# Shifting kinds of items against each other in one program order: a hybrid GLA / DeltaNet / MLA block on one core

## What is computed

```python
for l in range(DEPTH):                                  # DEPTH = 2
    h  = rmsnorm(x, norm_w) * (1 + scale) + shift       # scale, shift, gate from silu(c) @ ada_w
    p  = h @ w_in                                       # all branches' columns at once
    ya = gated_head_norm(bidirectional(gla_chunk_scan, ...), gla_norm_w, p['gla_z'])
    # GDN: 5-tap conv over tokens, silu, l2norm of q and k, then per chunk of 64 tokens
    #   t_inv = inverse(eye + strict_lower((k*beta) @ k.T * decay)); u = t_inv @ v_beta; w = t_inv @ ...
    #   v_new = u - w @ s;  o = q @ s + att @ v_new;  s = s * d + k.T @ v_new
    yb = gated_head_norm(bidirectional(gdn_chunk_scan, ...), gdn_norm_w, p['gdn_z'])
    yc = softmax(qn @ kn.T + qr @ kr.T) @ v * silu(p['mla_z'])        # low-rank q and kv
    x  = x + gate * (sum_i sigmoid(p['merge_gate'][i]) * (y_i @ w_branch[i])) @ w_out
```

## Time and profile before

| | us |
|---|---|
| median of 3 executions | 2361.31 (2359.95 to 2364.90) |
| the profiled execution's own time | 2353.64 |
| its span, first to last instruction | 2351.6 |
| TensorE busy | 2167.6 (92% of the span) |
| VectorE, ScalarE, GpSimd busy | 931.7, 846.4, 358.0 |
| mean granted TensorE clock | 0.969 |
| HBM traffic over the span | 80 GB/s |

### The profile page before, as it was taken

How to read it: one execution, slowest core, us unless ns; L and a number is a source line. 1 busy time by engine, 2 the same in 40 slices (tenths; PEclk the granted TensorE clock), 3 DMA queues, 4 the chain that set the end, 5 groups by cost and what they waited for, 6 DMA issues and landing times. The chain is left out here.

```text
span 2351.6 us, 31435 instructions
## 1 busy us (share of the span) xinstructions
PE 2167.6 (92%) x10970; PEld 1468.8 (62%) x10970; DVE 931.7 (40%) x2271; ACT 846.4 (36%) x2205; POOL 358.0 (15%) x591
## 2 busy tenths in 40 slices
PE   6999899899979989999999999988988968899998
PEld 3676576555545776555674437766575657766787
DVE  2023364656563325333331120246667653243321
ACT  2223253535443224444231112245346443244421
POOL 1000007071542000000000010000742760000000
PEclk8999899999989999999999999999999989999999
DMA  8215312211212022111222342122321312223243
GB/s 290 68 58 171 101 39 66 80 51 47 81 28 64 28 63 82 55 46 37 73 73 89 107 149 77 34 73 67 95 64 55 89 38 73 63 92 110 90 143 126
DMA packets 191419, 190.14 MB, mean 81 GB/s; under 512 B 28559, under 2 KB 185955, under 8 KB 190755
## 3 DMA queue, kind: packets, MB, share of 16 engines
q1 hardware_dynamic: 186048, 171.08, 23.5%
q0 software_dynamic: 3648, 16.72, 2.2%
q10 hardware_dynamic: 1571, 0.34, 0.1%
HBM read 178.62 MB, written 9.50 MB: 80 GB/s over the span
## 5 line engine op out<-in xcount | busy, mean ns | idle before, releaser
L1042 PE MATMUL bank<-hT,ring 128*128 128x512 f32 (+2 forms) x1856 | 727.1, 542 | 5.5 <-DMA ring<-in_w_in_dram 3.5
L1042 PEld LDWEIGHTS bank<-hT,ring 128*128 128x128 f32 (+1 forms) x1856 | 335.4, 192 | 256.1 <-issue 237.7
L1042 PE MATMUL bank<-ring,hT 128*128 128x256 f32 (+2 forms) x2112 | 458.5, 373 | 25.0 <-DMA ring<-in_w_in_dram 25.0
L1042 PE MATMUL bank<-WORK 128*128 128x128 f32 (+4 forms) x3056 | 403.7, 289 | 73.8 <-ACT WORK L1672 21.0
L1042 PEld LDWEIGHTS bank<-WORK 128*128 128x128 f32 (+3 forms) x3056 | 324.9, 172 | 188.9 <-issue 139.4
L1042 PEld LDWEIGHTS bank<-ring,hT 128*128 128x128 f32 x2112 | 385.8, 193 | 88.1 <-issue 35.6
L1042 PE MATMUL bank<-yT,ring 128*128 128x512 f32 (+1 forms) x768 | 273.4, 490 | 0.0
L1042 PEld LDWEIGHTS bank<-yT,ring 128*128 128x128 f32 x768 | 139.5, 193 | 80.2 <-issue 71.1
L1007 POOL TENSOR_TENSOR WORK<-WORK 64x31 f32<-64x31 f32 (+15 forms) x248 | 149.5, 603 | 19.4
L1977 DVE SCALAR_TENSOR_TENSOR WORK<-WORK,CW 128x512 f32<-128x512 f32 (+1 forms) x192 | 146.7, 764 | 3.0
L1005 POOL TENSOR_TENSOR WORK<-WORK 64x31 f32<-64x31 f32 (+15 forms) x248 | 139.5, 562 | 19.5
(11 more groups left out here) (202 smaller groups left out, 2071.0 us busy)
## 6 DMA issues: line engine op xcount, KB each, us to landing
ring<-in_w_in_dram SPq DMA_DIRECT2D x92, 1024.0 KB, 5.4
ring<-in_ada_w_dram SPq DMA_DIRECT2D x24, 1024.0 KB, 6.4
ring<-in_w_branch_dram SPq DMA_DIRECT2D x24, 1024.0 KB, 5.2
ring<-in_w_out_dram SPq DMA_DIRECT2D x8, 1024.0 KB, 5.0
ring<-in_mla_q_up_dram SPq DMA_DIRECT2D x8, 576.0 KB, 4.0
xs<-yT POOLq DMA_DIRECT2D x2, 2048.0 KB, 10.6
ring<-in_mla_kv_up_dram SPq DMA_DIRECT2D x8, 512.0 KB, 4.7
yT<-xs POOLq DMA_DIRECT2D x2, 2048.0 KB, 10.0
```

The source lines that it names most:

```text
L1042: return nc.tensor.matmul(o, a, b, start=start, stop=stop, skip_group_check=True)
```

## The change

A table gives some kinds of items a number, and the finished plan is sorted by position minus that number: a kind with 5 stands five positions ahead of its even place, one with -3 three behind. Items without an entry keep theirs, and equal keys stay in the old order. Keys that begin with v are for the VectorE part of a split kind. The banks, the ring and SyncE's issues are worked out from the new plan by the same rules. Besides, the first `gqk` product of a layer, which is woven with `lr`, now waits for its own block of shifted input by itself, as `lr` did; before, it relied on standing behind `lr`. The items are the same 2422, with the same instructions.

```diff
--- before.py
+++ after.py
@@ -149,6 +149,20 @@
 def pieces(it):
 
     return [("pc",) + it + (i,) for i in range(NPIECE[it[0]] - 1)] + [it]
+
+
+AHEAD = {'gw': 4, 'ga': 2, 'dnq': 3, 'yT': -2, 'cv': 4, 'ms': 2, 'mkv': 3, 'muk': -6, 'dx6': 3, 'dqkv': 5, 'd1': 1, 'muq': 2, 'dya': 3, 'vdn': -2, 'gv': 4, 'ab': 4, 'go': -3, 'dn': -1, 'mo': -8, 'vdsil2': 1, 'abT': -7, 'sq': -3, 'nx': 3, 'dy6': 3, 'dv': 1, 'dyb': 2, 'mod': -1}
+
+
+def settle(s):
+
+    def at(n):
+        it = s[n]
+        mark, it = (it[0], it[1:]) if it[0] == "v" else ("", it[1:-1] if it[0] == "pc" else it)
+        g = it[2] if it[0] in PHASE and PHASE[it[0]] < 2 and len(it) > 2 else 0
+        return n - AHEAD.get((mark + it[0], it[1], g), AHEAD.get(mark + it[0], 0))
+
+    return [s[n] for n in sorted(range(len(s)), key=lambda n: (at(n), n))]
 
 
 def schedule():
@@ -346,7 +360,7 @@
         if sums:
             s += sums[6:7] + [("mod", l + 1, 4)] + sums[7:] + [("modT", l + 1, 4), ("mod", l + 1, 5), ("modT", l + 1, 5)]
     s += [("xout", tt, h) for tt in tiles(DEPTH - 1) for h in range(2)]
-    return s
+    return settle(s)
 
 
 PHASE = {"lr": 0, "gqk": 0, "gv": 0, "ga": 0, "ge": 0, "gb": 0, "gatt": 0, "gw": 0, "go": 0,
@@ -760,6 +774,13 @@
                 else:
                     for who in READERS[b[0]]:
                         pe.wait_ge(*done(b, who))
+
+        def input_here(pe, l, kk):
+
+            if kk in SHIFTED_BY_DVE[l]:
+                pe.wait_ge(s_hd, shifted(l, kk, True))
+            else:
+                pe.wait_ge(s_ha, shifted(l, kk, False))
 
         def rows_of(u):
             return {"kup": KVL // P, "qup": QL // P}.get(u[0], KT)
@@ -1101,10 +1122,7 @@
                     w = weights(it)
                     n = KT // (last_piece + 1)
                     for kk in range(piece * n, piece * n + n):
-                        if kk in SHIFTED_BY_DVE[l]:
-                            pe.wait_ge(s_hd, shifted(l, kk, True))
-                        else:
-                            pe.wait_ge(s_ha, shifted(l, kk, False))
+                        input_here(pe, l, kk)
                         grp = kk % NGRP_LR
                         ins = mm(ps[grp * 32:(grp + 1) * 32, :], w[:, kk, :], hT[:, kk, :],
                                  kk < NGRP_LR, kk >= KT - NGRP_LR)
@@ -1123,6 +1141,8 @@
                     w = weights(it)[:, :, (j % 2) * P:(j % 2 + 1) * P]
                     n = KT // (last_piece + 1)
                     for kk in range(piece * n, piece * n + n):
+                        if k == "gqk" and it[2] == 0:
+                            input_here(pe, l, kk)
                         ins = mm(ps[:, a0:T], w[:, kk, :], src[:, kk, a0:T], kk == 0, kk == KT - 1)
                 elif k in ("gv", "z", "mkv", "mq"):
```

## The result

The changed kernel takes 2287.86 us (median of 4, 2285.61 to 2291.36) against 2360.63 for the kernel before (median of 4), 72.8 us less by the two medians. The prediction had 32 and a range that ended at 2300. The direction was right and the size wrong by a factor of two. In a later comparison on another chip the same kernel stood at 0.9728 (0.9713 to 0.9742), 64 us. One execution of the kernel with `mkv` alone, the one that was traced, took 2407 us at a mean clock of 0.922; it is left out of that kernel's ratio, and its trace is not read.

A forecast was written before the change was run, and what follows sets the result against it. TensorE was taken as the bound, its idle and low-clock time the only gain. Terms of 41 us gained less 9 lost made 32: 2321.6 us for a profiled execution, 2329 for the median, range 2300 to 2354.

The forecast's parts named there:

- Bound: Whole kernel: TensorE is the bound; only its idle and lower-clock time can be won, nothing between 1000 and 1390 us.
- Norm products: Conv products: waits before `dn` shrink 15.9, restarts 3.6; 4 lost before `d2`, 5 beside the solve; net 10.5 us gained.
- Loads: `w_in` loads: moving `mkv` ahead frees ring slots sooner for `mq` and `z`; 8 of 28.5 us gained.
- Tail before the scan: Head pair 2: the last silu and ScalarE's copy for the scan come sooner; 4.5 us gained.
- Inversion: Head pairs' inversion: `dy6` one filler further from `dx6` gains 3.6, `dya` behind `dx` loses 2; 1.5 us gained.
- MLA and yT: MLA: `mo` later gains 7.4, `mkT` loses 2.5, so 5 us gained; `yT` two places later gains 2.5.
- What gets later: New waits: `sq` behind `st` 2, `abT` near `dg` 1, `ab` at layer 1's GDN entry 3, unseen 3; 9 us lost.
- Clock: TensorE: four spells at lower clock follow waits that shrink, so they shrink too; 7 us gained.
- More goes than I count: Rival, chance 0.09: all norm waits, half the loads and more elsewhere vanish; 55 us gained, 2306 us.
- The waits only move: Rival, chance 0.23: TensorE, once earlier, meets the same head, solve or scan landings; 10 us gained, 2351 us.
- The slower one: Rival, chance 0.09: beside GpSimd's solve, VectorE's taps make the conv chain the bound, period above 8.60; 15 us slower, 2376.

The follow-up runs named there:

- the conv group: Only the six entries dqkv, cv, dnq, dn, v.dn, v.dsil2 in the table, against the kernel before: ratio 0.9882, 28 us gained.
- the inversion's entries: Only dx6 3, dy6 3, dyb 2, dya 3, dv 1, d1 1 in the table, against the kernel before: ratio 0.9956, 10 us gained.
- the last versions: Changed kernel with head pair 2's first `st` 12 ahead (both layers; layer 0 only; both, last silu chain 12 later): 0.9726, 0.9731, 0.9714 of before.
- `mo` and its neighbours: Only mo -8, muk -6, muq 2, ms 2 in the table, against the kernel before: ratio 0.9939, 14 us gained.
- the entry's four: Only ab 4, abT -7, nx 3, mod -1 in the table, against the kernel before: ratio 0.999 (0.9977 to 1.0002).

## Why the prediction was wrong in size

The mechanism held: TensorE's waits went where the plan moved them. The step that failed is the pricing of the terms. The idle time that the trace lists was taken for the whole price of a wait outside the norm products, loads were followed behind `mkv` alone, the inversion was priced for one of its steps, and 9 us of losses were put in that hardly came.

**Bound.** Right. TensorE's work did not change, the full stretch around 1000 to 1390 stayed full, and the gain came out of TensorE's waits but for a few us of clock.

**Norm products.** The mechanism and the net were right, two of the parts were not. The waits fell by 14.1 (forecast 15.9), with 0.23 more for each of the 15 that are gone (forecast 0.2), 3.5 us; the new wait before `d2` costs 6.5 (forecast 4), but 4.4 of it is one wait behind the solve's landing and not six of 0.7. The 5 us that were to come back beside the solve did not: here is `dn` in layer 1 while GpSimd is busy with a solve for 13.5 of 15 us (1806 to 1821).

```profile
1806.01 0.59 PE L1063 MATMUL bank<-RS,ONES 128*128 128x256 f32 x2
1813.31 0.59 PE L1063 MATMUL bank<-RS,ONES 128*128 128x256 f32 x2
1820.61 1.02 PE L1063 MATMUL bank<-RS,ONES 128*128 128x512 f32 x2
```

The period is 7.30, which is the 7.73 of the stretch without a solve less the 0.43 by which a `dn` of 256 columns is shorter. 14.1 + 3.5 - 6.5 = 11.1, against 10.5. The group made 28 and not 19. Of the excess the traces show 6 us, the loads behind `dqkv`; with the tail's 4.1 that sums to some 21, and the other 7 of the 28 have no place (the group's own trace is 24.4 us shorter than that of the kernel before).

**Loads.** The first term that failed. "8 gained of 28.5" was counted for `mkv` and for a piece or so of `z`. The list lost 16.1, of which 3.5 at the entry of layer 1 only changed its name: some 12.6 are gained. By place, one of the two waits at the start of MLA is gone in each layer, 7.2 us with what the other lost, where I had 5.5; and the two `z` waits among the conv products went from 3.78 and 7.95 to 1.77 and 4.63, 5.3 us, where I had 2.5. A kind that is the last user of a ring slot and moves ahead starts a load sooner. The runs show it for `mkv` and `dqkv`; I followed only `mkv`. `gv` moves ahead too, and no run shows what it did.

**Tail before the scan.** Right alone, wrong in company. With the conv group alone the scan's wait fell from 21.0 to 16.9, 4.1 us where 4.5 were forecast. In the whole change it stands at 20.0, and at 9.4 before `su` of layer 0, where it was 9.2: the inversion's entries bring TensorE there sooner too (24.0, 24.4 and 26.2 us of this wait in the three kernels that have them without the conv group), to a chain on ScalarE and VectorE that ends when it ends. And what is won there is mostly taken back by the solve behind it, as the last versions show.

**Inversion.** The second term that failed: "1.5 gained", measured 10 by the two kernels with these entries. In the trace after, 8.5 us are left (6.1 and 2.4) where 19.4 stood.

**MLA and yT.** The third: 5 and 2.5, plus 8 for loads. `mkv` gave 12 (interval 8 to 17), of which the loads by place are 7.2. `mo` and its neighbours gave 14: `mo`'s 7.4 was all gained as forecast, the 2.5 before `mkT` was mostly not lost, and part of the rest is what a wait costs beyond its idle time. `yT`'s 2.5 was 3.5 by the list.

**What gets later.** The fourth: 9 us of losses (`sq` 2, `abT` 1, `ab` 3, unseen 3). The runs with these entries alone lose nothing: `sq` 0, the entry's four 2 us gained if anything. The loss that did come, `d2`, was priced in its own place.

**Clock.** Some 4 us by the two traces against 7, and some 7 if the trace of the empty table, the same plan as before with a clock of 0.968, is taken for the kernel before. It can't be told from chance: see the last section.

**The method.** I took the idle time before a record as the price of a wait and added 0.2 for restarting to one family of waits alone. The trace shows 46.3 us less idle time and 15.8 less busy time for the same records, of which some 4 is clock: about 11 us that stood in no list, and the 42 waits fewer at 0.23 each account for 10 of it. The Trainium skill (Perfetto Trace Analysis, "Identifying the Most-Contended Engine") says that the busy share of TensorE's matmuls is no good measure of how close a kernel is to its roofline, because pipelined instructions look smaller in the trace. The trace agrees in that the same 10970 records were busy for 2167.6 and then 2151.8 us, and that records of 7.03 us in all make way for the next one after 6.87.

**The rivals.** "More goes than I count" was the right one, at 2306, and too small as well. "The waits only move" holds in three places: between `su` and the solve, at the entry of layer 1, and at the first solve of layer 1, where 4.4 us stand before `d2`. The slower one never came near its point of decision, 8.60 us: the taps did slow down beside the solve (two in 2.05 at 670 us, where 0.75 each is the price alone), but VectorE, at 41% of the span, had the room. The Trainium skill (SBUF — State Buffer, "SBUF: two separate sides") says that a VectorE operation with two SBUF inputs and a GpSimd one that reads SBUF block each other on a shared pair of ports. The tap's 1.02 agrees with it; that the chain would then set the pace did not follow.

```profile
670.51 2.05 DVE L1997 SCALAR_TENSOR_TENSOR WORK<-WORK,CW 128x512 f32<-128x512 f32 x2
```

## What to carry to other kernels

Price a wait by the distance between the starts of the work before and after it, compared with the same work where it does not wait, and not by the idle time before a record: here a wait of 0.64 us cost 0.87, and over the kernel some 57 us went, the clock's 4 or so taken off, where 46 were listed. When items move in a shared order, follow every kind that frees a buffer, for its move starts a load even where no wait of its own is at stake. Look at what an item that moves back comes to stand behind: `v.dn` came behind a step that waits for the solve. When a wait is gone from the list, see whether another has grown beside it. And before a large wait is worked on, look for the next fixed landing behind it: here 15 of the 20 us before `su` went and at most a few us of time, no more than the intervals allow, because a solve on another engine lands when it lands.

## What was not expected of the hardware

A wait of 0.64 us costs 0.87 in each of the periods shown, though no record is longer for it: 0.16 of the rest is the overlap of two records that falls away.

And the clock does not take the same course each time at the same place in the same order. The kernel with `sq` alone has the plan of before up to the heads. This is the stretch of 150 us at the end of GLA and the start of the conv products (for `sq`'s kernel shifted by the 3 us that it started later; span, TensorE's busy us and records, clock, DMA share, GB/s), of the kernel before and of `sq`'s:

```profile
195.00:345.00 150.00, 136.10 (x695) 0.92 0.39 122
```

```profile
198.00:348.00 150.00, 136.40 (x727) 0.95 0.39 122
```

The same order gave 32 records more in the same time, at a clock of 0.95 instead of 0.92; 0.03 of 150 us is 4.5. The kernels with the empty table and with `dn` alone repeated the slower course; the one with the inversion's entries, whose plan is the same up to there too, had 0.97 (199 to 349 us). So a gain of 5 us at this place in a single trace, the changed kernel's too, may be chance, and the clock term of 7 can't be judged from one pair of traces. The medians carry the result, and the traces the places.
